# Output products of a gated linear attention as 64 by 64 tiles of TensorE

## What is computed

```python
def gla_chunked(q, k, v, log_decay):          # C = 64, n = 256 // 64 = 4
    gcs = jnp.cumsum(log_decay.reshape(b, n, C, H, dk), axis=2)
    ref = gcs[:, :, C // 2:C // 2 + 1]
    scores = jnp.einsum('bnihd,bnjhd->bnhij', q * jnp.exp(gcs - ref), k * jnp.exp(ref - gcs))
    scores = jnp.where(causal, scores, 0.0)
    o_intra = jnp.einsum('bnhij,bnjhv->bnihv', scores, v)
    ...
    o_inter = jnp.einsum('bnihd,bnhdv->bnihv', q * jnp.exp(gcs), prev_states)
    return (o_intra + o_inter).reshape(b, L, H, dv)
```

## Time and profile before

| | us |
|---|---|
| median of 3 runs | 1795.35 |
| lowest and highest of them | 1794.28, 1800.11 |
| the profiled execution | 1794.72 |
| its span | 1793.0 |

### The profile page before, as it was taken

The page is one execution under the profiler, slowest core; times in us unless marked ns, Lnnn a source line. Parts: engine busy times, 40 slices in busy tenths (PEclk is TensorE's granted clock), DMA queues, the critical chain, the costliest instruction groups (busy, mean ns, idle before and its releaser), DMA issues.

```text
span 1793.0 us, 25753 instructions
## 1 busy us (share of the span) xinstructions
PE 1756.5 (98%) x9143; PEld 1487.9 (83%) x9143; DVE 1412.5 (79%) x1583; ACT 1159.1 (65%) x1414; POOL 91.6 (5%) x140
## 2 busy tenths in 40 slices
PE   7999999999999999999999999999999999999998
PEld 7988888897888888888888888888888897878986
DVE  8854454697998998999989999899999786636555
ACT  5544444464877777777777777777777565534554
POOL 0000000002800000000000000000000001000000
PEclk9999999999999999999999999999999999999999
DMA  9555555544999999999999999999999543325520
GB/s 336 169 172 195 190 179 195 180 141 165 358 381 374 389 373 351 374 379 386 376 346 395 394 345 387 341 348 378 369 366 383 201 136 125 133 95 165 163 95 36
DMA packets 211714, 486.92 MB, mean 272 GB/s; under 512 B 13397, under 2 KB 14628, under 8 KB 211636
## 3 DMA queue, kind: packets, MB, share of 16 engines
q1 hardware_dynamic: 209840, 480.02, 74.8%
q0 software_dynamic: 1152, 4.19, 0.6%
q10 hardware_dynamic: 644, 1.63, 0.3%
HBM read 482.67 MB, written 3.15 MB: 271 GB/s over the span
## 4 chain that ended last, share of the span: by engine, by line
PE 92%; DVE 5%; ACT 1%; issue 1%; DMA 0%; ACTq 0%; POOL 0%; DVEq 0%; POOLq 0%
PE ps L1850 84%; DVE wlo L1060 2%; PE ps L2141 1%; DVE arena L1518 1%; PE ps L2370 0%; ACT whi L535 0%; PE ps L2103 0%; PE ps L2104 0%; PE ps L2293 0%; PE ps L1942 0%; PE ps L1994 0%; DVE arena L1051 0%; PE ps L2366 0%; PE ps L2307 0%; PE ps L2037 0%
## 5 line engine op out<-in xcount | busy, mean ns | idle before, releaser
L1060 DVE TENSOR_TENSOR wlo<-raw,whi 128x1024 fp32r<-128x1024 f32 x910 | 1070.1, 1220 | 258.4 <-ACT whi L535 257.9
L535 ACT ACTIVATE whi<-raw 128x1024 fp32r<-128x1024 f32 x910 | 913.2, 1053 | 456.6 <-PE ps L1850 454.6
L1850 PE MATMUL ps<-whi,ya 128*128 128x512 f32 x2272 | 727.0, 393 | 3.0 <-DVE ya L1051 1.8
L1850 PEld LDWEIGHTS ps<-whi,ya 128*128 128x128 f32 x2272 | 426.8, 188 | 91.4 <-DVE ya L1051 2.0
L1850 PE MATMUL ps<-wlo,ya 128*128 128x512 f32 x1136 | 442.7, 390 | 0.0
L1850 PE MATMUL ps<-whi,yh 128*128 128x512 f32 x896 | 285.7, 390 | 0.0
L1850 PEld LDWEIGHTS ps<-wlo,ya 128*128 128x128 f32 x1136 | 213.6, 188 | 42.5
L1850 PEld LDWEIGHTS ps<-whi,yh 128*128 128x128 f32 x896 | 168.3, 188 | 35.6 <-issue 0.6
L1850 PE MATMUL ps<-hhi,whi 128*128 128x256 f32 x656 | 188.2, 287 | 2.5 <-DVE hlo L1122 1.8
L1850 PE MATMUL ps<-hlo,whi 128*128 128x256 f32 x656 | 185.7, 283 | 0.0
L1850 PE MATMUL ps<-hhi,wlo 128*128 128x256 f32 x656 | 185.7, 283 | 0.0
(11 more groups left out here) (366 smaller groups left out, 1184.4 us busy)
## 6 DMA issues: line engine op xcount, KB each, us to landing
raw<-in_moe_w_gate SPq DMA_DIRECT2D x112, 1024.0 KB, 6.7
raw<-in_moe_w_up SPq DMA_DIRECT2D x112, 1024.0 KB, 7.2
raw<-in_moe_w_down SPq DMA_DIRECT2D x112, 1024.0 KB, 6.8
raw<-in_even_w_in SPq DMA_DIRECT2D x21, 1024.0 KB, 5.2
raw<-in_w_in SPq DMA_DIRECT2D x20, 1024.0 KB, 5.8
raw<-in_odd_w_in SPq DMA_DIRECT2D x16, 1024.0 KB, 5.5
raw<-in_ffn_w_gate SPq DMA_DIRECT2D x14, 1024.0 KB, 5.2
raw<-in_ffn_w_up SPq DMA_DIRECT2D x14, 1024.0 KB, 5.1
```

The source lines that it names most:

```text
L535: act.activation(hi_of(u)[:, n], raw[:, c % RAW, n], ACT.Copy).then_inc(w_hi, 1)
L1060: dve.tensor_tensor(lo_of(u)[:, n], raw[:, c % RAW, n], hi_of(u)[:, n].bitcast(F32), ALU.subtract).then_inc(w_lo, 1)
L1850: ins = pe.matmul(o, s, m, start=first and n == 0, stop=last and n == 2, skip_group_check=True)
```

## The change

`gla_out(i)` computes all score products of a set first, each head's two chunks as two products of 64 by 64 (stationary) with 128 moving columns, in the diagonal tiles of the array (rows and columns 0 to 63, and 64 to 127). The last of them counts up a new semaphore g_own, and TensorE waits for it. Then come the state products: 64 rows (row half r) and the 64 columns of chunk m only, written to the partitions of chunk m. The PSUM flag `start` stands only at the first product of each bank and half. As no zero columns of Q4 are read, GpSimd no longer fills it, DVE no longer waits for that (q4_zero), and GpSimd's wait for s_xdt1 ahead of the fill goes too. SCT is still filled with zeros.

```diff
@@ GpSimd
                     pool.wait_ge(sem("s_skip"), 1)
-                    pool.wait_ge(sem("s_xdt1"), 1)
-                    pool.memset(Q4, 0.0).then_inc(sem("q4_zero"), 1)
                     pool.wait_ge(sem("s_yq"), 8)
@@ DVE
             dve.wait_ge(sem("g_e"), 5)
-            dve.wait_ge(sem("q4_zero"), 1)
@@ TensorE, gla_out
+                sub = (slice(0, 64), slice(64, 128))
                 for q in range(4):
+                    c = slice(P * q, P * (q + 1))
                     for r in range(2):
-                        pr = slice(64 * r, 64 * r + 64)
-                        o = ps[:, 6 + r, P * q:P * (q + 1)]
                         hh = 2 * q + r
-                        pe.matmul(o, SCT[i][:, 512 * r + P * q:512 * r + P * (q + 1)], V[:, i, P * hh:P * (hh + 1)], start=True, stop=False)
                         for m in range(2):
-                            n = 2 * i + m
-                            if n:
-                                ins = pe.matmul(o, Q5[pr, q, i, m, :], S1[n][pr, P * q:P * (q + 1)], start=False, stop=m == 1)
+                            first = 512 * r + P * q + 64 * m
+                            ins = pe.matmul(ps[sub[m], 6 + r, c], SCT[i][sub[m], first:first + 64], V[sub[m], i, P * hh:P * (hh + 1)],
+                                            start=q == 0, stop=2 * i + m == 0 and q == 3, skip_group_check=True)
+                ins.then_inc(sem("g_own"), 1)
+                pe.wait_ge(sem("g_own"), i + 1)
+                for q in range(4):
+                    c = slice(P * q, P * (q + 1))
+                    for m in range(2):
+                        n = 2 * i + m
+                        if n:
+                            for r in range(2):
+                                ins = pe.matmul(ps[sub[m], 6 + r, c], Q5[sub[r], q, i, m, sub[m]], S1[n][sub[r], c], start=False, stop=q == 3,
+                                                skip_group_check=True)
                 ins.then_inc(sem("g_o"), 1)
```

## The result

The changed kernel takes 1785.32 us in the median of 6 runs (1784.95 to 1786.92), against 1795.44 for 6 runs of the kernel before (1794.28 to 1800.11). The ratio is 0.994, with a 95% interval of 0.9928 to 0.9951. By it, 1795.35 becomes 1784.6 (1782.4 to 1786.6). Its profiled execution took 1784.95 us, with a span of 1783.2, 9.77 less than the profiled execution before.

A forecast was written before the change was run, and what follows sets the result against it. TensorE, busy 98% of the span, bounds the kernel. Savings of 3.42 us in the first set and 5.18 in the second, 8.6 in all, take 1794.72 to 1786.1, plus 0.63 for the median: 1786.8, range 1784.8 to 1793.0.

The forecast's parts named there:

- the likeliest case: Both sets of output products: score products in pairs, second set's state products in four tiles; 1786.8 us, chance 0.42.
- T(n) = 0.20 + 0.11 n: TensorE time in us for n records in one tile, from a run's first record to the next shape's first.
- Rival C: Score phase: two tiles writing one PSUM bank run in turn, 1.76 us more in each set; 1790.3 us, chance 0.12.
- State products: Products after the wait in each set: 8 records for each tile, 1.08 us; in the second set four tiles at once.
- A: Output products: pairs in the score phase, four tiles in the second set's state phase; 1786.8 us, chance 0.42.
- B: Second set's state phase: never more than two tiles at once, 0.88 us less saved; 1787.6 us, chance 0.24.
- The shorter weight loads: First load of each of four phases is shorter at 64 columns, 0.05 us each; 0 to 0.2, taken as 0.
- The fill: GpSimd's fill of Q4, 1.81 us at 1491.5: nobody waited for it, so removal gains 0 to 1.8, taken as 0.
- The 0.80 and the 1.10: TensorE's waits in us, before the second set for DVE's state and before the transposes for DVE L1697; both unchanged.
- The ten microseconds in hand: ACT and DVE have this slack before the chain to the transposes, so that chain moves with TensorE.
- how the numbers follow: Prediction's step giving chances, faster 0.67, same 0.24, slower 0.09, likeliest time 1786.8 us and range 1784.8 to 1793.0.
- the smaller wake: TensorE's restart after waiting on its own semaphore: lower bound 0.1 us more for a set, where 0.2 was taken.

The follow-up runs named there:

- the experiment with only the order: Kernel before, with only each set's order changed: score products first (128 by 128), the wait, then state products of 128 columns; 1787.29 us, ratio 0.994.
- both orders tried: Changed kernel with the second set's state products ordered by chunk, 1786.47 us; changed kernel with score products ordered by tile, 1787.84 us.

## Where the prediction was right, and where it failed

The mechanism, the sign and the likeliest case were right; the size was too small and the lower edge too high. By the ratio of the runs, 0.994 of 1795.35, the time is 1784.6, and that is 0.2 below the range (1784.8 to 1793.0). The median, 1785.32, lies half a microsecond inside it, and the ratio's interval (1782.4 to 1786.6) reaches to both sides of the edge. The forecast saving was 8.6 us; measured are 9.0 in the sets, 9.8 between the two profiles, 10.1 between the medians and 10.8 by the ratio.

- **What a record costs.** The 0.11 of T(n) = 0.20 + 0.11 n held, with 0.109 a record in 64 by 64 tiles. The 0.20 held for products of 128 columns (1.10 us for eight records a tile in the experiment with only the order, T(8) = 1.08). With 64 columns it came as 0.15 (1.02).
- **Score products.** Expected at T(16) = 1.96 and 0.2 for the wait, 2.16 from the first score record to the first state record; measured 2.03 (1574.28 to 1576.31). Rival C did not come true: in the score phase two row halves wrote one PSUM bank, in different partitions, at the same time, two records starting within 0.01 us of each other. The Trainium skill, TensorEngine Tiling (Array Packing), section Restrictions and Gotchas, says that different row tiles cannot access one PSUM bank at the same time. Read strictly, this trace does not agree.
- **State products.** Expected 1.08, measured 1.02 (1576.31 to 1577.33) and 1.04 (1590.82 to 1591.86). All four tiles at once, which no row before showed, is settled for A against B.
- **The sets.** Expected 3.24 each, measured 3.05 and 3.06; the saving was 8.97, not 8.60. Two terms of the sum were off. The shorter weight loads, taken as 0 with 0 to 0.2 in the range, gave the whole 0.2: in each of the four phases the second record starts 0.16 us after the first, not 0.21. The wait, taken as 0.2 more for a set, cost 0.14: 0.34 us between the starts around it, where a change of shape alone has 0.20. The rest, about 0.05, is 0.109 instead of 0.11 for a record.
- **The fill.** Worth 0, as expected.
- **What is late next.** The 0.80 and the 1.10 stayed. The ten microseconds in hand carried the whole saving.
- **The step that failed is the last, how the numbers follow: the base that the sum is taken from, and the lower edge.** The sum's own terms were 0.37 us short. More of the miss lies in a term that stood at nothing without a reason: how the time outside the sets differs from run to run. It has two parts. First, the stretch ahead of the sets: there 0.77 us lie between the two profiles, and the first set began between 1574.08 and 1576.20 in the profiles of kernels that are alike up to there except for the fill, a spread of 2.1 us, where the edit gave 9. Second, the highest of the three runs shown, 1800.11. The prediction names it as spread and does not ask what it is. Of such runs of the kernel before one was profiled (1799.68), and its 5 us more are a fall of the clock that begins within the second set. In the changed kernel none of 18 runs lies over 1786.92. How much of the 10.8 the ratio owes to such runs was not measured.
- **The lower edge was also added up wrongly.** The three terms named for it are 0.2 for the weight loads, 1.8 for the fill and 0.1 a set for the smaller wake, 2.2 in all. From 1786.8 that gives 1784.6 and not 1784.8, and 1784.6 is what was measured. To hit it so would have been luck, since 1.8 of the 2.2 is the fill, which was worth 0.

## What to carry to other kernels

Where small matmuls of different shape alternate, look at the distance of their starts first: here each change of shape cost 0.2 us beside 0.11 for a record, and putting products of one shape together gave 7.8 of 9.0 us, before any zero was saved. A part of it, about 2.6 by estimate, came because products of different row halves then stood side by side and ran at once. Let consecutive products go to different tiles in turn, since TensorE looked only three records per busy tile ahead for an idle one. And before a range is written, ask of the highest run shown in which stretch it could have lost its time.

## What the runs showed of the hardware that I had not expected

- Four 64 by 64 tiles ran at once at 0.11 us for four fp32 records (state phase of the second set); there each row half wrote a bank of its own. In the score phase two tiles in different row halves wrote one PSUM bank at once, in different partitions, also at 0.11 us for a pair of records.
- TensorE starts work for an idle tile past work for a busy one, when three records of each busy tile are still to come, in both orders tried.
- The granted clock fell to 1.2 GHz for 13 us, beginning inside a stretch of alternating shapes. From 1560 to 1590 TensorE had counted as busy throughout, and its only idle time after that was the 0.81 us ahead of the set. It cost 5 us. 14 of the 60 runs of the kernel before that are listed beside the kernels of this study lie near 1800 us, and one of them was profiled. For 13 of the 14 the mean granted clock is known: it is 0.989 to 0.991, and 0.992 to 0.996 in the 41 other runs of that kernel for which it is known. So these runs all had a lower clock, but in which stretch was seen in one alone. What brings the clock down, the alternation or the 0.81 us wait ahead of it, was not shown. For the alternation speaks that the changed kernel has the wait as before and no alternation, and its 18 runs have no such case. Against it, the ten runs with small state products in the old order have none either, though they still alternate, if for 6.24 us in the second set instead of 8.42.
